# One decoder layer in float32: side-by-side halves in the third projection's matmuls, and the first projection's loop written out

## What is computed

```python
proj = x @ w_in                                   # 2048 -> 6432 columns
y_rwkv = rwkv7_mixer(proj[..., :RWKV_COLS], ...)  # 16 heads x 64, recurrent
y_diff = diff_attention(proj[..., RWKV_COLS:], ...)  # 8 heads, 128-wide values
mix = concatenate([y_rwkv, y_diff], -1) @ w_out
x = layer_norm(ALPHA * x + mix)
h = square(relu(x @ w_ff1)) @ w_ff2               # 2048 -> 8192 -> 2048
x = layer_norm(ALPHA * x + h)
```

## Time and profile before

| | |
|---|---|
| three runs | 1343.86, 1345.84, 1346.96 us |
| the profiled execution | 1345.55 us, span 1343.8 us from first to last instruction |
| TensorE busy, mean granted clock | 1284.4 us (96%), 0.988 |
| VectorE busy | 721.3 us (54%) |
| ScalarE busy | 572.8 us (43%) |
| GpSimd busy | 95.9 us (7%) |
| loads | 215.68 MB, 162 GB/s over the span |

### The profile page before, as it was taken

How to read it: one execution, slowest core, us unless ns; L and a number is a source line. 1 busy time by engine, 2 the same in 40 slices (tenths; PEclk the granted TensorE clock), 3 DMA queues, 4 the chain that set the end, 5 groups by cost and what they waited for, 6 DMA issues and landing times.

```text
span 1343.8 us, 26747 instructions
## 1 busy us (share of the span) xinstructions
PE 1284.4 (96%) x11224; PEld 1163.7 (87%) x11224; DVE 721.3 (54%) x726; ACT 572.8 (43%) x618; POOL 95.9 (7%) x65
## 2 busy tenths in 40 slices
PE   6999999999899879999999999999999999999995
PEld 6899989998788857878999999999988888888884
DVE  5366757673644316667444444444455555655557
ACT  4744445443445222444333333333344444444443
POOL 0011202060000010019200000000000000000000
PEclk9999999999999988999999999999999999999998
DMA  8245444552000153563555555555565555555541
GB/s 332 104 161 188 161 157 170 180 180 82 3 4 3 37 220 125 191 247 129 185 188 187 177 176 181 184 187 187 172 254 194 192 188 188 190 190 191 195 171 62
DMA packets 32808, 218.91 MB, mean 163 GB/s; under 512 B 4677, under 2 KB 5061, under 8 KB 6878
## 3 DMA queue, kind: packets, MB, share of 16 engines
q1 hardware_dynamic: 32734, 217.80, 46.4%
HBM read 215.68 MB, written 2.10 MB: 162 GB/s over the span
## 4 chain that ended last, share of the span: by engine, by line
PE 88%; DVE 7%; ACT 3%; issue 2%; DMA 0%; DVEq 0%; SPq 0%; ACTq 0%
PE ps L427 87%; DVE wlo L1253 2%; ACT whi L965 1%; PE ps L659 1%; DMA stage<-w_in 0%; DVE stats L1568 0%; DVE xres L1671 0%; DVE x1f L1603 0%; ACT L965 0%; DVE xres L1567 0%; DVE xres L1669 0%; ACT xres L965 0%; ACT kr L965 0%; PE ps L542 0%; DVE sm L1411 0%
## 5 line engine op out<-in xcount | busy, mean ns | idle before, releaser
L1253 DVE TENSOR_TENSOR wlo<-stage,whi 128x2048 fp32r<-128x2048 f32 x192 | 449.9, 2343 | 483.6 <-ACT whi L965 483.1
L965 ACT ACTIVATE whi<-stage 128x2048 fp32r<-128x2048 f32 x194 | 371.6, 1915 | 622.9 <-PE ps L427 619.9
L427 PE MATMUL ps<-acthi,whi 128*128 128x256 f32 x1712 | 490.7, 287 | 18.3 <-DVE wlo L1253 14.9
L427 PE MATMUL ps<-actlo,whi 128*128 128x256 f32 x1712 | 486.5, 284 | 2.3 <-issue 2.3
L427 PE MATMUL ps<-acthi,wlo 128*128 128x256 f32 x1712 | 486.2, 284 | 0.0
L427 PEld LDWEIGHTS ps<-acthi,whi 128*128 128x128 f32 x1712 | 330.4, 193 | 21.6 <-issue 18.3
L427 PEld LDWEIGHTS ps<-actlo,whi 128*128 128x128 f32 x1712 | 330.5, 193 | 4.5 <-issue 4.5
L427 PEld LDWEIGHTS ps<-acthi,wlo 128*128 128x128 f32 x1712 | 330.4, 193 | 0.0
L427 PE MATMUL ps<-whi,shi 128*128 128x512 f32 x632 | 248.9, 394 | 1.2 <-DVE slo L1540 1.2
L427 PE MATMUL ps<-whi,slo 128*128 128x512 f32 x632 | 247.1, 391 | 0.0
L427 PE MATMUL ps<-wlo,shi 128*128 128x512 f32 x632 | 247.1, 391 | 0.0
(11 more groups left out here) (212 smaller groups left out, 898.2 us busy)
## 6 DMA issues: line engine op xcount, KB each, us to landing
stage<-w_ff SPq DMA_DIRECT2D x128, 1024.0 KB, 4.8
stage<-w_in SPq DMA_DIRECT2D x51, 1024.0 KB, 4.9
stage<-w_out SPq DMA_DIRECT2D x16, 1024.0 KB, 4.9
xstage<-xT SPq DMA_DIRECT2D x4, 512.0 KB, 7.1
xres<-x SPq DMA_DIRECT2D x1, 2048.0 KB, 7.7
gain<-ln_gain SPq DMA_DIRECT2D x2, 1024.0 KB, 6.7
bias<-ln_bias SPq DMA_DIRECT2D x2, 1024.0 KB, 8.8
out<-xres SPq DMA_DIRECT2D x8, 256.0 KB, 2.1
```

The costliest lines, as they stand in the source:

```text
L427: return pe.matmul(out, lhsT, rhs, start=start, stop=stop, skip_group_check=True)
L965: return act.activation(out, in_, func, **kw)
L1253: TTn(wlo[k0 % NHL][:, :], stage[k0 % NST][:, :], f(whi[k0 % NHL][:, :]), ALU.subtract).then_inc(s_lo, 1)
```

## The change

`acthi` and `actlo` become two views of one tile `acts` [128, 16, 2, 256], so that the rounded values and the remainders of a block stand side by side. A new function `both` issues two matmuls in place of three: one of 512 columns, `whi` by both halves, into a whole PSUM bank, and one of 256 columns, `wlo` by the rounded half, into the first half of the bank. The third projection uses it in all its chunks (in the first one directly, in the others by `pairs`). The first projection and the value projection keep their matmuls.

A bank of the third projection then holds two partial results. ACT copies the second half into `hid` (it took the Relu of the only one before), DVE adds the first half to it and raises `s_sum`, waits for that, and then takes max(h, 0) * h in one scalar_tensor_tensor and raises `s_ff`. TensorE waits on `s_sum` where it waited on `s_ff`.

The loop of the first projection is written out in Python on TensorE, ACT and DVE, so its instructions stand there twice, with fixed addresses and wait values. POOL's loop stays. The kernel's other loops stay.

```diff
--- before.py
+++ after.py
@@ -123,8 +123,8 @@
         stage = [at(f"stage{i}", i, [P, SLAB]) for i in range(NST)]
         whi = [at(f"whi{i}", 4 + i, [P, SLAB], F32R) for i in range(NHL)]
         wlo = [at(f"wlo{i}", 6 + i, [P, SLAB], F32R) for i in range(NHL)]
-        acthi = at("acthi", 8, [P, KT, S], F32R)
-        actlo = at("actlo", 10, [P, KT, S], F32R)
+        acts = at("acts", 8, [P, KT, 2, S], F32R)
+        acthi, actlo = acts[:, :, 0, :], acts[:, :, 1, :]
 
         wup = at("wup", 12, [65, RW])
         aup = at("aup", 12, [P, RW], byte=4096)
@@ -267,7 +267,7 @@
         s_pg = sem("ln_gained_pool")
         s_xt, s_x1h, s_x1f, s_x1l = sem("x1_transposed"), sem("x1_hi"), sem("x1_scaled"), sem("x1_lo")
         s_x1v = sem("x1_lo_vector")
-        s_relu, s_ff = sem("relu_ready"), sem("hidden_ready")
+        s_low, s_sum, s_ff = sem("low_half_copied"), sem("hidden_summed"), sem("hidden_ready")
 
         block = ctx.enter_context(nc.Block())
 
@@ -430,6 +430,20 @@
                 pe.wait_ge(s_hi, g + 1)
                 pe.wait_ge(s_lo, g + 1)
 
+            def both(bank, w, cols, k):
+
+                mm(ps[:, bank, :], whi[w][:, cols], acts[:, k, :, :].rearrange("p h q -> p (h q)"), start=(k == 0),
+                   stop=False)
+                return mm(ps[:, bank, 0:S], wlo[w][:, cols], acthi[:, k, :], start=False, stop=(k == KT - 1))
+
+            def pairs(b0, g, k0):
+                for s in range(2):
+                    halves_ready(g + s)
+                    for j in range(8):
+                        for fb in range(2):
+                            last = both(b0 + fb, (k0 + s) % NHL, slice(256 * j + fb * P, 256 * j + fb * P + P), 8 * s + j)
+                    last.then_inc(s_used, 1)
+
             def chunk(b0, g, k0, width=256, slabs=2, ready=None):
 
 
@@ -494,7 +508,7 @@
                                   cst[:, C_SU:C_SU + 2 * P])
                     last.then_inc(s_item, 1)
 
-            with pe.Fori(0, NB // 4) as i:
+            for i in range(NB // 4):
                 for jj in range(2):
                     for c in range(PER):
                         m, k0 = PER * jj + c, G_MIX + 2 * (PER * jj + c)
@@ -910,21 +924,17 @@
                     else:
                         pe.wait_ge(s_x1v, k - POOL_LOWS + 1)
                     for fb in range(2):
-                        acc = ps[:, fb, 0:S]
-                        cols = slice(256 * j + fb * P, 256 * j + fb * P + P)
-                        mm(acc, whi[w][:, cols], acthi[:, k, :], start=(k == 0), stop=False)
-                        mm(acc, whi[w][:, cols], actlo[:, k, :], start=False, stop=False)
-                        last = mm(acc, wlo[w][:, cols], acthi[:, k, :], start=False, stop=(k == KT - 1))
+                        last = both(fb, w, slice(256 * j + fb * P, 256 * j + fb * P + P), k)
                 last.then_inc(s_used, 1)
-            chunk(2, G_FF1 + 2, G_FF1 + 2)
+            pairs(2, G_FF1 + 2, G_FF1 + 2)
             with pe.Fori(1, N_FF1 // 2) as i:
                 for k in range(2):
-                    pe.wait_ge(s_ff, i * 2 + (k - 1))
-                    chunk(2 * k, i * 4 + (G_FF1 + 2 * k), G_FF1 + 2 * k)
+                    pe.wait_ge(s_sum, i * 2 + (k - 1))
+                    pairs(2 * k, i * 4 + (G_FF1 + 2 * k), G_FF1 + 2 * k)
 
             NG = DFF // P // 4
             for h in range(2):
-                pe.wait_ge(s_ff, N_FF1 - 1 + h)
+                pe.wait_ge(s_sum, N_FF1 - 1 + h)
                 g0 = h * NG // 2
                 for n in range(4 * g0, 4 * g0 + 4):
                     pe.wait_ge(s_ahi, KT + n + 1)
@@ -1018,7 +1028,7 @@
             A(cosb[:, :], angt[2][:, :], ACT.Sin).then_inc(s_sin, 1)
 
             hi(G_MIX + 1, G_MIX + 1)
-            with act.Fori(0, NB // 4) as i:
+            for i in range(NB // 4):
                 for jj in range(2):
                     for c in range(PER):
                         m, k0 = PER * jj + c, G_MIX + 2 * (PER * jj + c)
@@ -1200,7 +1210,7 @@
                 if not last:
                     hi(i * 4 + (k0 + 3), k0 + 3)
                 act.wait_ge(s_used, i * 4 + (k0 + 2))
-                A(hid[:, bass.ds(i * 4 + 2 * k, 2), :], ps[:, 2 * k:2 * k + 2, 0:S], ACT.Relu).then_inc(s_relu, 1)
+                A(hid[:, bass.ds(i * 4 + 2 * k, 2), :], ps[:, 2 * k:2 * k + 2, S:2 * S], ACT.Copy).then_inc(s_low, 1)
 
             with act.Fori(0, N_FF1 // 2 - 1) as i:
                 for k in range(2):
@@ -1313,7 +1323,7 @@
             dve.wait_ge(s_sin, 2)
             dve.wait_ge(s_gam, 1)
             lo(G_MIX + 1, G_MIX + 1)
-            with dve.Fori(0, NB // 4) as i:
+            for i in range(NB // 4):
                 for jj in range(2):
                     def pair(x, o=0):
                         return x[:, bass.ds(i * 4 + (2 * jj + o), 2), :]
@@ -1621,9 +1631,11 @@
                 lo(i * 4 + (k0 + 2), k0 + 2)
                 if not last:
                     lo(i * 4 + (k0 + 3), k0 + 3)
-                dve.wait_ge(s_relu, i * 2 + (k + 1))
+                dve.wait_ge(s_low, i * 2 + (k + 1))
                 h2 = hid[:, bass.ds(i * 4 + 2 * k, 2), :]
-                TTn(h2, ps[:, 2 * k:2 * k + 2, 0:S], h2, ALU.mult).then_inc(s_ff, 1)
+                TTn(h2, ps[:, 2 * k:2 * k + 2, 0:S], h2, ALU.add).then_inc(s_sum, 1)
+                dve.wait_ge(s_sum, i * 2 + (k + 1))
+                STT(h2, h2, 0.0, h2, ALU.max, ALU.mult).then_inc(s_ff, 1)
 
             with dve.Fori(0, N_FF1 // 2 - 1) as i:
                 for k in range(2):
```

## The result

Five executions of the changed kernel took 1324.91, 1325.06, 1333.04, 1334.42 and 1336.89 us: a median of 1333.04 us against 1345.88 us before (five executions). The ratio is 0.9882 with a 95% interval of 0.9835 to 0.9929, so the change makes the kernel faster: by 15.9 us by the ratio (9.6 to 22.2 by its interval), and by 12.8 us in the medians. The forecast was 1327.0 us, the range 1323.5 to 1334.0. The sign and the range held, but the median lies 6 us above the forecast and only 1 us inside the range, and the five times fall into two groups. That is what the experiments had to explain.

A forecast was written before the change was run, and what follows sets the result against it. TensorE, busy 96% of the span, was taken to bound the kernel through its matmul pitch. Savings of 12.9 us (pairs) and 5.8 us (loop) sum to 18.7 us, giving a median of 1327.0 us, range 1323.5 to 1334.0.

The forecast's parts named there:

- The loop, 5.8 us: First projection: writing out the loop removes one jump back with its stops and half clock, saving 5.8 us (2.5 to 7.1).
- Rival 1: First projection: the stop belongs to that point of the program and stays, giving 1332.9 us; chance 0.10.
- The pairs, 12.9 us: Third projection: two matmuls replace three, 0.347 us a pair instead of 0.360, saving 12.9 us over 992 pairs.
- The prediction's own sign of being wrong: Third projection: a pair taking above 0.350 us would show the prediction wrong.
- The bounds, 10.9 to 13.4: Third projection: limits in us on the pairs' saving, from joined matmul pitches of 0.229 and 0.2265 us.
- Rival 2: Third projection: the joined matmul costs 0.237 us instead of 0.227, so pairs save 3.0 us, total 1337; chance 0.06.
- What was costed at nothing: Third projection: DVE's extra operation, ACT's Copy, TensorE's wait for the sum and the stage's end (bound 0.5 us) cost nothing.
- The first chunk's pairs: Third projection: 32 pairs left out of the saving, since TensorE waits there for DVE's wlo anyway.
- Rival 3: Third projection: longer DVE or ACT work delays slabs by 0.1 to 0.4 us for part, 1329 to 1338 us; chance 0.04.
- the prediction's second sign of being wrong: Third projection: a TensorE wait for DVE inside the stage would show the prediction wrong.
- The slower rival: Third and fourth projections: other loops begin to pay up to 5.8 us per jump, 1466 us with all 24; chance 0.03.

The follow-up runs named there:

- e2: The kernel before with only the first projection's loop written out on TensorE, ACT and DVE; median 1338.91 us, ratio 0.9939.
- e4: The changed kernel with the first projection's loop put back on TensorE alone; median 1338.9 us of three executions, ratio 0.993 to the kernel before.
- f1: The changed kernel with 512-column matmuls first, then 256-column ones, per third-projection slab from the second chunk on; median 1329.43 us, ratio 0.9863 to the kernel before.
- g1: f1 with grouping in the first projection too, and the wait for remainders moved between the groups; median 1319.87 us, ratio 0.979 to the kernel before.
- e1_after: The changed kernel measured again, nothing edited; median 1334.45 us, ratio 0.9884 to the kernel before.
- g2: The changed kernel with four more 65x256 DVE operations behind each chunk's square in the third projection; median 1333.9 us, ratio 0.9892 to the kernel before.
- f3: The changed kernel with TensorE's third-projection loop in three passes of ten chunks (640 matmuls) instead of fifteen of two; median of two 1334.57 us.
- g3: The kernel before with TensorE's third-projection loop in three passes of ten chunks (960 matmuls) instead of fifteen of two; median 1354.14 us, ratio 1.0044.
- g4_after: The changed kernel measured a third time, nothing edited; median 1334.04 us, ratio 0.9896 to the kernel before.

## Why the prediction was right, and where it was not

**The bound.** TensorE's matmul pitch sets the time in both places: shown, by F - C, which is 992 times the pitch to within half a microsecond, and by V.

**The loop, 5.8 us.** Right in size and in mechanism. Written out alone it moves V by 6.2 us (e2), put back on TensorE alone it brings 5.9 to 6.7 us back (e4, against the three traces of the changed kernel). That the jump stands behind both stops was argued from the earlier trace rows; it is now shown. Rival 1, to which I gave 0.10, falls.

**The pairs, 12.9 us.** This is the step that failed, in its size. The sum took 0.227 us for the joined matmul from the earlier trace rows and 0.120 for the narrow one from the earlier trace rows. Each of those rows is from a stream of one size, and the sum assumed that they can be added in a stream that alternates. In the short pattern they can, by chance (0.3467); in the long one the pair costs 0.3533 us, and the term is 992 x 0.0067 = 6.6 us instead of 12.9. The prediction's own sign of being wrong, a pair above 0.350 us, stands in five of the seven traces. The bounds, 10.9 to 13.4, held only matmuls with equal neighbours, though the prediction says itself that the trace of before has no row of the new kind: they should have reached down to a pair that saves little. Rival 2 had the right form (the pair costs more than 0.347), with a chance of 0.06 and a price of 10 ns where 6.6 were measured. f1 shows that the joined matmul has its 0.227 us and that the long pattern needs the alternating order: with sizes grouped the stage took 345.4 us (345.1 in g1), without it. That f1's executions also stayed within 3.5 us is no proof of its own, since C - V could have spread them.

**The sum.** 5.8 + 6.6 gives 12.4 us, and 1345.9 - 12.4 = 1333.5 us, where the median lies (1333.04). 5.8 + 12.9 gives 1327, and the two shortest executions, 1324.9 and 1325.1, are near that; the second is the traced one, in the short pattern. Between the first trace and e1_after the pattern makes 6.3 us and C - V 6.0 us. That the slower three of the first five executions ran in the long pattern is likely (five of seven traces did) but not shown, since only one of the five was traced. So it is partly luck that the range held: its upper end was set by rival 1, which fell, the median lies 1 us under it, and the same kernel again gave medians of 1334.45 and 1334.04 us, just above it, beside a kernel before that was some 2.5 us slower there.

**What was costed at nothing.** DVE's square: 0.69 us against a forecast of 0.7, with 1.84 us of pause behind it, of 1.95 forecast, and 1.3 us more put in there brought three waits, of 0.5, 0.5 and 0.9 us (g2). At the stage's end 0.39 us were left, 0.3 forecast. TensorE never waits for the sum. The first chunk's pairs are worth nothing, as said: TensorE still waited for wlo before C. Rival 3 did show, but small: beside POOL's work the square took 1.07 us and wlo up to 3.44 us, and in six of the seven traces a wlo came late at least once in the stage, in the changed kernel by 0.14 to 0.19 us at the fourth slab. By itself that is nothing, but it is a wait of TensorE for DVE inside the stage, the prediction's second sign of being wrong, and in e1_after, e4 and f3 the long pattern, worth 6 us, begins right behind it.

**The slower rival.** Other loops did not begin to pay, though the written-out code shifts their place: no gap at a jump in the third projection of any trace with the short body. That a jump in another loop can cost is shown by g3, but there the length of the body does it, with 960 matmuls in a pass: two jumps of 3.6 us each made the kernel before slower by 0.44%.

**The page on the fixed cost per matmul.** The Trainium skill, "TensorE: Matmul & The Clock Gate", section "Wait — 56ns, not 53.3ns?", gives a warm matmul about 2.5 ns over its columns, by which the pairs would save 2.5 us (an estimate by that page). The runs don't agree: F - C fell by 6.7 or 13.0 us, so for this stream the figure is too small in both patterns.

**Left open.** What decides which way a restart goes: the same program, waiting at the same slab for about the same time, went on short in the first trace and in g4_after and long in e1_after. The distances in the long pattern look like two rhythms that meet every three pairs, but no run tells which, and no run took the late wlo away while the sizes alternate. Why wlo is slower beside POOL in the changed kernel (3.44 us) than in the one before (2.53) is open too.

## What to carry to other kernels

A pitch measured in a stream of one matmul size is not the pitch in a stream that alternates; group equal sizes, and measure several executions before believing one trace. Look at the distances between starts as well as at the waits: a wait of 0.2 us that no list of waits held stood where 6 us began to be lost. Put the matmuls that need an operand last behind a wait of their own, after those that don't. And keep a loop's body on TensorE short or write it out: a jump back was free over 640 matmuls and cost 3.6 to 6 us over 960 in this kernel.

## What the runs showed of the hardware that I had not expected

- The same stream of 512- and 256-column matmuls runs at one of two steady rates, 0.3467 or 0.3533 us a pair, at full granted clock. It changed from one to the other only at a restart after a wait, one of 0.13 to 0.16 us being enough (e1_after, e4_pe_loop, f3_body10), and then kept it for over 300 us.
- A jump back of TensorE cost nothing over 192 or 640 matmuls and stopped it for about 2 us over 960, once or twice, with the 1.2 GHz level behind the stop (granted clock 0.51).
- In the stages where TensorE pauses, its stretches at half clock fall in other places in each execution: five of them and 327.2 us between V and C in the first trace, eight and 333.2 us in e1_after.
